# Expert mixers from f32 weight buffers in blocks of 32 rows, and row loads ahead of weights in the first stage

## The reference

```python
def block_ffn(args):
    e, idx = args                     # one expert, 128 slots
    xb = h_pad[idx]                   # gathered rows of 1024
    return (jax.nn.silu(xb @ w1[e]) * (xb @ w3[e])) @ w2[e]
```

```
layer 0: 26 39 3 368 | 12 28 20 238 | 73 18 29 163 | 16 55 4 247 | 37 18 23 322 | 122 28 14 64 | 9 3 15 80 | 17 23 26 420
layer 1: 52 80 41 48 | 49 57 89 86 | 33 52 27 50 | 52 92 72 96 | 46 62 51 81 | 59 62 65 86 | 41 79 40 79 | 68 66 65 122
```

## Time and profile before

| | us |
|---|---|
| median of three runs | 3011.33 (3010.84 to 3011.63) |
| profiled execution | 3014.36 |
| its span | 3012.5 |
| `front` | 0 to 76.6 |
| `route` and `experts` of layer 0 | 688.9 to 1526.3 |
| `route` and `experts` of layer 1 | 2277.2 to 2932.95 |
| last stage, `combine` | 2932.95 to the end |

### The profile page before, as it was taken

One profiled execution on the slowest core, in us unless ns is written; L12 is line 12 of the kernel. 1 busy time (PEld: TensorE's weight loads), 2 busy tenths in 40 slices (PEclk: granted clock), 3 DMA queues, 4 the chain that ended last, 5 costly groups with the idle time before them and its releaser, 6 DMA issues. The chain is left out here.

```text
span 3012.5 us, 41138 instructions
## 1 busy us (share of the span) xinstructions
PE 2510.7 (83%) x13498; PEld 2036.1 (68%) x13498; DVE 1993.3 (66%) x2023; ACT 1449.3 (48%) x1624; POOL 346.5 (12%) x400
## 2 busy tenths in 40 slices
PE   6788761993999999999929989979694999999970
PEld 3567651883788888888818867768583788888850
DVE  3779998665767777688336203357665888888855
ACT  3210011551666666677234213367321777777742
POOL 1000001000001000011012110053100111111104
PEclk7789885995999999999969999989795999999985
DMA  7354332223798888899464321034553999999956
GB/s 273 126 169 141 127 140 73 87 98 108 296 340 317 320 312 298 321 389 388 159 217 171 119 64 28 8 114 169 208 179 101 382 389 387 390 386 390 398 212 224
DMA packets 292015, 679.43 MB, mean 226 GB/s; under 512 B 22974, under 2 KB 49934, under 8 KB 291912
## 3 DMA queue, kind: packets, MB, share of 16 engines
q1 hardware_dynamic: 261564, 575.75, 52.9%
q0 software_dynamic: 20064, 66.16, 6.5%
q10 hardware_dynamic: 10284, 36.16, 3.0%
HBM read 588.01 MB, written 90.00 MB: 225 GB/s over the span
## 5 line engine op out<-in xcount | busy, mean ns | idle before, releaser
L1497 DVE TENSOR_TENSOR moe_w_lo<-moe_w_raw,moe_w_hi 128x2048 fp32r<-128x2048 f32 x384 | 862.4, 2286 | 88.1 <-ACT moe_w_hi L1426 50.2
L1426 ACT ACTIVATE moe_w_hi<-moe_w_raw 128x2048 fp32r<-128x2048 f32 x384 | 714.3, 1909 | 66.9 <-issue 39.5
L100 PE MATMUL moe_pg<-moe_w_hi,moe_xt_hi 128*128 128x512 f32 x592 | 243.7, 412 | 11.5 <-DVE moe_xt_lo L1508 5.9
L100 PE MATMUL moe_py<-moe_w_hi,moe_at_hi 128*128 128x512 f32 x592 | 241.7, 408 | 11.9 <-DVE moe_w_lo L1497 8.2
L101 PE MATMUL moe_pg<-moe_w_lo,moe_xt_hi 128*128 128x512 f32 x592 | 237.2, 401 | 0.0
L102 PE MATMUL moe_pg<-moe_w_hi,moe_xt_lo 128*128 128x512 f32 x592 | 236.9, 400 | 0.0
L101 PE MATMUL moe_py<-moe_w_lo,moe_at_hi 128*128 128x512 f32 x592 | 235.0, 397 | 0.0
L102 PE MATMUL moe_py<-moe_w_hi,moe_at_lo 128*128 128x512 f32 x592 | 234.8, 397 | 0.0
L102 PE MATMUL moe_pu<-moe_w_hi,moe_xt_lo 128*128 128x512 f32 x592 | 234.3, 396 | 0.0
L100 PE MATMUL moe_pu<-moe_w_hi,moe_xt_hi 128*128 128x512 f32 x592 | 234.1, 396 | 0.0
L101 PE MATMUL moe_pu<-moe_w_lo,moe_xt_hi 128*128 128x512 f32 x592 | 234.1, 396 | 0.0
(11 more groups left out here) (367 smaller groups left out, 5445.0 us busy)
## 6 DMA issues: line engine op xcount, KB each, us to landing
moe_w_raw<-in_moe_w SPq DMA_DIRECT2D x384, 1024.0 KB, 12.8
taps_ada_w<-in_ada_w SPq DMA_DIRECT2D x40, 1024.0 KB, 7.0
scratch_experts_out<-moe_y ACTq DMA_DIRECT2D x57, 512.0 KB, 6.4
taps_raw<-in_conv_pw_w SPq DMA_DIRECT2D x20, 512.0 KB, 9.4
scan_v<-scratch_gla_values SPq DMA_DIRECT2D x20, 512.0 KB, 4.1
front_w<-in_ada_w SPq DMA_DIRECT2D x8, 1024.0 KB, 18.9
cv_raw<-in_gla_w_in SPq DMA_DIRECT2D x16, 512.0 KB, 3.9
scratch_gla_out<-scan_o SPq DMA_DIRECT2D x16, 512.0 KB, 6.6
```

The source lines that it names most:

```text
L100: pe.matmul(out, xh, wh, start=start, stop=False)
L1426: act.activation(hi[m][:, cut, :], raw[m][p][:, cut, :], ACT.Copy).then_inc(s(f"{m}_hi{h}"), 1)
L1497: dve.tensor_tensor(lo[m][:, cut, :], raw[m][p][:, cut, :], hi[m][:, cut, :].bitcast(F32), ALU.subtract).then_inc(s(f"{m}_lo{h}"), 1)
```

## The change

In `front` SyncE loads the rows, eight tiles ahead of all weights and the last two behind the first part of `ada_w`; the units stand behind tiles 6 and 8 and, the last two, behind all tiles. In `conv_taps` ScalarE issues one DMA that writes 4 MB of zeros over the experts' output slots past the first 2560. `route` works with blocks of 32 rows, keeps its tables in the last weight buffer, and SyncE starts the weights of the first three experts in it. In `experts` nothing is split into high and low parts. Four buffers hold the whole f32 weights of an expert each. For a block, 128 pieces of 1 KB are gathered (32 tokens in four strips), the 32 rows are the stationary operand, and each strip of 32 array columns takes another quarter of the weight's columns, 256 at a time. TensorE's program has one body for each of the four buffers, and in it a loop over the expert's further blocks. The other engines loop over blocks, four bodies per turn.

```diff
-GROUPS, PER_GROUP, EXPERTS, FF, BLK = 4, 8, 32, 512, 128
+GROUPS, PER_GROUP, EXPERTS, FF, BLK = 4, 8, 32, 512, 32
 front:
-        unit_behind = {1: 0, 4: 1, 7: 2, 9: 3}
+        unit_behind = {6: 0, 8: 1}
+                for t in range(LAT_TILES):
+                    load(t)                       # on SyncE, was on GpSimd
                 for q in range(4):
...
+                    if q == 0:
+                        for t in range(LAT_TILES, TILES):
+                            load(t)               # waits for "scaled" of tile t - 8
 conv_taps, ScalarE, at pair n == 1:
+                            act.dma_start(d.yd[2 * TOK:, :].rearrange("(p r) (s n) -> p (r s) n", p=P, n=D // 4),
+                                          zeros[:, :].unsqueeze(1).to_broadcast([P, EXPERTS * BLK // P * 4, D // 4]))\
+                                .then_inc(s("covered"), 16)
+class Feed:
+    BUFS, AHEAD = 4, 3
...
+    def load_pair(self, sp, x):
+        e, b = EXPERT_ORDER[x], x % self.BUFS
+        for m, src in enumerate((self.d.w1, self.d.w3)):
+            for h in range(2):
+                sp.dma_start(self.pair[:, b, m, h * KC // 2:(h + 1) * KC // 2, :].rearrange("p (s c) n -> p s (c n)", c=2),
+                             src[self.layer, e, h * D // 2:(h + 1) * D // 2, :].rearrange("(s p c) n -> p s (c n)", p=P, c=2))\
+                    .then_inc(self.sem(f"pair_loaded{b}"), 16)
 route, SyncE and TensorE:
+                for x in range(feed.AHEAD):
+                    feed.load_pair(sp, x)
+                    feed.load_back(sp, x)
-                    last = pe.matmul(pi[:, :], in_slot[:, j, :], in_blk[:, j, :], start=j == 0, stop=j == 2 * nt - 1)
+                    for r in range(0, P, BLK):
+                        last = pe.matmul(pi[r:r + BLK, :], in_slot[:, j, :], in_blk[:, j, :],
+                                         start=j == 0, stop=j == 2 * nt - 1)
 experts, SyncE:
+                for x in range(EXPERTS):
+                    times = x // BUFS + 1
+                    sp.wait_ge(feed.sem(f"pair_loaded{x % BUFS}"), 64 * times)
+                    sp.sem_inc(s("pair_ready"), 1)
+                    sp.wait_ge(feed.sem(f"back_loaded{x % BUFS}"), 32 * times)
+                    sp.sem_inc(s("back_ready"), 1)
+                    if 1 <= x < EXPERTS - feed.AHEAD:
+                        done = sp.value_load(plan.ends[0:1, x - 1:x], min_val=1, max_val=nb)
+                        sp.wait_ge(s("pair_done"), done)
+                        feed.load_pair(sp, x + feed.AHEAD)
+                        sp.wait_ge(s("back_done"), done)
+                        feed.load_back(sp, x + feed.AHEAD)
 experts, TensorE:
+                def out_product(out, buf):
+                    for c in range(STRIPS):
+                        for j in range(STRIPS):
+                            last = pe.matmul(out[j * BLK:(j + 1) * BLK, 0:CUT], at[:, c * BLK:(c + 1) * BLK],
+                                             feed.back[:, buf, c, j * CUT:(j + 1) * CUT], start=c == 0, stop=c == STRIPS - 1)
+                    last.then_inc(s("back_done"), 1)
+                def in_product(k, b):
+                    for c in range(KC):
+                        for j in range(STRIPS):
+                            last = pe.matmul(pg[j * BLK:(j + 1) * BLK, 0:2 * P].rearrange("t (m n) -> t m n", m=2),
+                                             xt[:, c % 2, (c // 2) * BLK:(c // 2 + 1) * BLK],
+                                             feed.pair[:, b, :, c, j * P:(j + 1) * P], start=c == 0, stop=c == KC - 1)
+                    last.then_inc(s("pair_done"), 1)
+                    turn_x(k + 1)                 # two transposes of 128x128
+                def before_out(k, experts_in, b):
+                    if started(k, 1):
+                        pe.wait_ge(s("at_ready"), k)
+                        pe.wait_ge(s("back_ready"), experts_in)
+                        pe.wait_ge(s("y_out"), k)
+                        out_product(py, b)
+                    pe.wait_ge(s("a_ready"), k + 1)
+                    pe.transpose(pat[:, 0:P], a[:, :], ident[:, :]).then_inc(s("at_turned"), 1)
+                def expert(x, b, first):
+                    pe.wait_ge(s("xt_ready"), first + 1)
+                    pe.wait_ge(s("pair_ready"), x + 1)
+                    in_product(first, b)
+                    end = pe.value_load(plan.ends[0:1, ds(x, 1)], min_val=1, max_val=nb)
+                    before_out(first, x, (b - 1) % BUFS)
+                    with pe.If(first + 1 < end):
+                        with pe.Fori(first + 1, end) as k:
+                            pe.wait_ge(s("xt_ready"), k + 1)
+                            in_product(k, b)
+                            before_out(k, x + 1, b)
+                    return end
...
+                with pe.Fori(1, EXPERTS // BUFS) as i:
+                    end = pe.value_load(plan.ends[0:1, ds(i * BUFS - 1, 1)], min_val=1, max_val=nb)
+                    for b in range(BUFS):
+                        end = expert(i * BUFS + b, b, end)
 experts, ScalarE, VectorE and GpSimd, for block k:
+                    act.activation(sil[:, :], pg[:, 0:P], ACT.Silu).then_inc(s("sil_ready"), 1)
+                    take_x(k + 1)                 # xt: 128x256 out of PSUM
...
+                        act.activation(y[b][:, :], py[:, 0:CUT], ACT.Copy).then_inc(s("y_out"), 1)
+                    bring_x(k + 1, i + (p + 1) // UNROLL, (p + 1) % UNROLL)   # copies 128x256, waits for the gather
+                    dve.tensor_tensor(a[:, :], sil[:, :], pg[:, P:2 * P], ALU.mult).then_inc(s("a_ready"), 1)
+                    dve.tensor_copy(at[:, :], pat[:, 0:P]).then_inc(s("at_ready"), 1)
+                    pool.wait_ge(s("x_here"), k + 1)
+                    gather(k + UNROLL, p)
```

More of the change, by code:

```diff
@@ new lines, in route @@
+        before = sb([P, P])
+        ones = sb([P, P])
+        iota = sb([P, P])
+        token = sb([P, TILES])
+        strip = sb([P, 1])
+        gm = sb([P, nt])
+        ga = sb([P, nt, GROUPS])
+        gsel = sb([P, nt, GROUPS])
+        gw = sb([P, nt])
+        inner = [sb([P, nt, EXPERTS]) for j in range(2)]
+        cand = sb([P, nt, EXPERTS])
+        least = sb([P, nt])
+        top = sb([P, 2, nt])
+        hot = sb([P, 2, nt, EXPERTS])
+        both = sb([P, nt, EXPERTS])
+        sofar = sb([P, nt + 1, EXPERTS])
@@ L1031, in route @@
+        rank = sb([P, nt, EXPERTS])
+        picked = sb([P, 2, nt, EXPERTS])
+        mine = sb([P, 2, nt])
+        first = sb([P, 2, nt])
+        over = sb([P, 2, nt])
+        need = sb([P, EXPERTS])
+        ends = [sb([P, EXPERTS]) for j in range(2)]
+        in_slot = sb([P, 2 * nt, BLK])
+        in_blk = sb([P, 2 * nt, nb + AHEAD_X])
         pr = ph.ps("pr", [P, nt * EXPERTS])
         pa = ph.ps("pa", [P, nt * EXPERTS])
-        pi = ph.ps("pi", [P, nb + 1])
-        pb = ph.ps("pb", [1, P])
+        pi = ph.ps("pi", [P, nb + AHEAD_X])
@@ L1226, in experts @@
-        pu = ph.ps("pu", [P, FF])
-        pat = ph.ps("pat", [P, FC, P])
-        py = ph.ps("py", [P, D])
-        def blocks(eng, body, tail=None, otherwise=None):
-            count = eng.value_load(plan.block[0:1, nb:nb + 1], min_val=plan.fewest, max_val=nb)
-            for k in range(2):
-                body(k, k)
-            with eng.Fori(1, nb // 2) as i:
-                for p in range(2):
-                    k = i * 2 + p
+        ident = ph.sb("ident", [P, P])
+        idx = ph.sb("idx", [P, UNROLL], I32)
@@ L1241, in blocks @@
+        cut_rows = d.hd.rearrange("t (s n) -> (t s) n", n=CUT)
+        def blocks(eng, body, tail=None):
+            count = eng.value_load(plan.block[0:1, 0:1], min_val=plan.fewest, max_val=nb)
+            for k in range(UNROLL):
+                body(k, 0, k)
+            with eng.Fori(1, nb // UNROLL) as i:
+                for p in range(UNROLL):
+                    k = i * UNROLL + p
                     with eng.If(k < count):
-                        body(k, 2, i, p)
-                    if otherwise:
-                        with eng.If(k >= count):
-                            otherwise(k)
+                        body(k, i, p)
@@ L1322, in _ @@
-                sp.wait_ge(s("zero_set"), 1)
-                blocks(sp, body, lambda count, last: bring(("w2",), last, 1), None if layer else unused)
+                for x in range(feed.AHEAD, BUFS):
+                    feed.load_pair(sp, x)
+                    feed.load_back(sp, x)
+                for x in range(EXPERTS):
[10 more added lines that the diff above has]
+                        feed.load_back(sp, x + feed.AHEAD)
@@ L1548, in experts @@
+                bring_x(0, 0, 0)
+                blocks(dve, body)
+        ph.sems.update(feed.sems)
         ph.close()
```

571 lines of the change are left out of this document (211 added, 360 removed).

## The result

The changed kernel takes 2970.94 us (median of 4 runs, 2965.58 to 2974.41), the kernel before 3011.09 us beside it: a ratio of 0.9864, 95% interval 0.9851 to 0.9878. It is 40 us faster where 164 were forecast. The direction and the range (2780 to 2990) held; the size did not.

A forecast was written before the change was run, and what follows sets the result against it. TensorE, the only engine never resting in both expert stages, was taken as the bound. Layer 0 -111, layer 1 -47, front -10, zeros +2 make -166 against 3014.4: 2848, stated as 2847 us; range 2780 to 2990.

The forecast's parts named there:

- the price of the stores in the stream: Expert stages: gathers and stores, 30% added for short pieces, make a layer 0 expert's load 18.3 us instead of 15.7.
- Block 6.0 us: Experts: TensorE takes 6.0 us per block of 32 rows, four strips overlapping fully; bounds 5.5 and 11.2.
- Rivals 1 and 3: Experts: 1, block longer than its products, 7.4 us, chance 0.18; 3, strips overlap only in pairs, 11.2 us, chance 0.04.
- Announcements, 18 and 17 us: Expert stages: SyncE signals landed weights late, in program order, costing 18 us in layer 0 and 17 in layer 1.
- First product of layer 0 at 739: Start of layer 0's experts: first gather ends the wait, first product at 739 us instead of 743.
- Waits of TensorE between light experts, 75 to 90 us in layer 0: Sign in layer 0: TensorE waits for SyncE 75 to 90 us in all, longest before experts 25 to 31.
- Stream of layer 1, 17.3 us an expert: Layer 1 experts: weights with 2.5 blocks' gathers and stores take 17.3 us per expert, 554 us for 32.
- Code that isn't there (rival 2): TensorE's expert loop: jumps wait for instruction fetch, 246 us a layer, net +160 and +185, total 3195 us; chance 0.11.
- End of the experts to the next stage, 10 and 9 us: Behind the experts: 10 us to the next stage in layer 0, as before the change, and 9 to `combine` in layer 1.
- Front -10: First stage: rows loaded first shorten TensorE's wait for weights, -10 us, bounds 0 and -14.
- the stream decides: Layer 1 experts: weight loads, not 474 us of TensorE work, set the end; 2886 for 2933 us, -47.
- rival 1: Experts: a block takes longer than its products, 7.4 us; +90 and +35 us, total 2975 us; chance 0.18.

The follow-up runs named there:

- direct4: Changed kernel with each block's store cut into four DMAs and TensorE waiting on the weights' own semaphores instead of SyncE's announcements; 2841.74 us, ratio 0.9429 to the kernel before.
- store4: The cut store: changed kernel with each block's store issued as four DMAs of 32 partitions x 1 KB, same bytes and places; 2881.31 us, ratio 0.9564 to the kernel before.

## Why the prediction was wrong in size

**The step that failed is the price of the stores in the stream.** It was put as "with the blocks' gathers and stores in 1 KB pieces (0.26 MB a block, three blocks an expert, and 30% more for short pieces, an estimate)": bytes over 16 engines with a surcharge. The price came out of the size of the pieces, the real one out of how many engines carry them. From 2500 to 2600 us of the changed kernel q10 has

```profile
DMA packets 10441, 34.74 MB, mean 347 GB/s; under 512 B 738, under 2 KB 2367, under 8 KB 10441
...
q1 hardware_dynamic: 8138, 31.37, 88.3%
...
q10 hardware_dynamic: 1679, 1.67, 4.7%
```

and 4.7% of 16 engines is 19% of four. What is cut into equal parts over 16 engines goes at the pace of these four: an estimate of 0.81 x 410 = 333 GB/s for weights and gathers. Measured are 331 (34.74 MB less the stores' 1.67 in 100 us). This row of the profile would have given the loss, had the four been known. What it cost: 676 - 614 = 62 us in layer 1 and 788 - 759 = 29 in layer 0, 91 of the missing 124. In layer 1, 48 of the 62 are rest of TensorE (88.7 us against 40.9) and 15 are products at the lower clock (515 us busy against 500).

**A second step had no price at all**: that TensorE works slower after each wait. The forecast let it wait 88 us in layer 0 and took every block at full clock. With the cut store its 96 blocks still take some 24 us more than at 6.15 us each, in `direct4` some 19. The 24 us are read from records; no run takes them away alone.

The other terms, each as forecast and as measured:

- *Block 6.0 us*: 6.15 at full clock. The four strips overlap fully, as forecast: 3.66 us for the first products (3.44 + 0.14), 1.93 for the second (1.72 + 0.14). In 96 blocks that is 14 us too little. Rivals 1 and 3 (7.4 and 11.2 us) fall.
- *Announcements, 18 and 17 us*: 20 and 18, by `direct4`. This step was right, mechanism and size; and it had been left in the kernel as a cost, where one edit takes it out.
- *First product of layer 0 at 739*: the sum counts `front` apart, so this is 50 us behind the first issue of `route`, and it took 55 (731.40 - 676.20). The wait that ends last is for the identity, not for the gather.
- *Waits of TensorE between light experts, 75 to 90 us in layer 0*: 81.7. That the sign came true is luck: the longer loads are in it, and with the cut store, whose loads are near the forecast's, the waits are 59.0.
- *Stream of layer 1, 17.3 us an expert*: this number comes out of the prediction's own terms only without its 30% for short pieces; with it 17.8, 16 us more in the layer. With the cut store the measured load is 17.0: no surcharge shows. (The last line too is off by its own terms: 2848 less 3 is 2845, not 2847.)
- *Code that isn't there (rival 2)*: 9.3 us of "issue" before `pg` in layer 0, 5 times, and 21 more code packets. The mechanism may exist at that size; it was priced at 246 us a layer. The Trainium skill's window in "Runtime: NRT & Kernel Launch", instruction fetch mechanics, had the loop just fit, and these rows agree.
- *End of the experts to the next stage, 10 and 9 us*: 18.6 and 16.4. 5 us of each are the empty turns, by `tail4`.
- *Front -10*: -10.0 alone by the medians, 14 in the profile.

Layer 0 of the changed kernel, in terms that add up: 5 us more to the first product, 44 more of busy TensorE (14 the block, 30 the clock), 4 more of rest, 9 more at the end, 62 in all.

The forecast's reading of layer 1, "the stream decides", was right, and that is why the mistake weighed so much there: with the cut store the layer takes 614 us, forecast 609. Part of that closeness is luck: the stream was quicker than forecast (545 us against 554), and what stands behind it longer (67 us from the last landing to the next stage, against 52). The range held the result only through rival 1, a slower block, which is not what happened.

## What to carry to other kernels

Before pricing a DMA by its bytes, look at the first dimension of its two access patterns: a small store on few engines takes its share of the time from every large load that is spread over all of them (here 5% of the bytes, 15% of the rate). The signs in a profile are a DMA share near 1 at a rate below what the same stream reaches elsewhere in the run, and a plateau at a fraction of the rate when the stream ends; multiply the small queue's share by 16 over the number of its engines to see whether it explains the gap. And where a queue's engine gives signals in the order of its issues, let the consumer wait for the transfer's own semaphore: it was worth 20 and 18 us beside the cut store, 25 and 13 beside the whole one. And a wait of TensorE costs more than its length: the products behind it ran at a lower clock.

## What the runs showed of the hardware

- Four strips of 32 columns with 256 moving ones overlap fully: 64 f32 records in 3.66 us, 0.057 each, where one record alone takes 0.215.
- Stores on the same few engines by two shapes cost the same to 0.1 us at equal pieces per engine (3173.77 and 3173.71). From 32 to 64 pieces per engine and block the cost is not double but more than three times (from 90 to 292 us above `store4`); ScalarE's issues then last up to 9.6 us, where they lasted 1.1 at most.
- Behind stores with a first dimension of 4 the stream's end comes at about 102 GB/s, a quarter of 410; with a first dimension of 2 at about 50, an eighth.
- Behind stands of 4.1 to 5.6 us TensorE's next 64 records took 5.3 to 6.4 us at a granted clock of 0.56 to 0.68, for 3.66 at 1.00.
- In 4 KB pieces, with stores over all 16 engines, one core's stream holds 408 GB/s over 440 us.
- Empty turns of a loop are on the path at the end of a stage: ScalarE stood 6.6 and 6.3 us before the last copy, 2.7 and 3.0 (a true wait) without them, and the end of each stage came 5 us sooner.
